# Retention's value projection: two 256-column units in one pass of 512-column products, with the weight loads and sums around it reordered

## What is computed

```python
c_act = jax.nn.silu(c)
for l in range(DEPTH):
    mod = c_act @ w_ada[l] + b_ada[l]          # adaLN: shift, scale, gate
    h = _modulate(_rmsnorm(x, norm_mix_g[l]), shift1, scale1)
    p = h @ w_in                               # rq, rk, rv, rg, ...
    ...
# per retention head: q, k are 256 wide, v and gate 512 wide
q, k = rotary(rq), rotary(rk)
scores = (q @ k.T) * decay                     # causal
o = scores @ v
o = (o - mean(o)) * rsqrt(var(o) + GN_EPS)
y_a = (silu(rg) * o) @ w_ret_out
```

## Time and profile before

| | before |
|---|---|
| median of 3 runs | 2310.23 us (2309.91 to 2310.75) |
| profiled execution, its own time | 2309.64 us |
| span from first to last instruction | 2307.9 us |
| PE busy | 2283.3 us, 99% |
| POOL busy | 1141.3 us, 49% |
| DVE busy | 1082.2 us, 47% |
| ACT busy | 906.9 us, 39% |
| DMA queue of SP, share of 16 engines | 33.4% |
| granted TensorE clock | 1.000 over the span |

### The profile page before, as it was taken

How to read it: one execution, slowest core, us unless ns; L and a number is a source line. 1 busy time by engine, 2 the same in 40 slices (tenths; PEclk the granted TensorE clock), 3 DMA queues, 4 the chain that set the end, 5 groups by cost and what they waited for, 6 DMA issues and landing times.

```text
span 2307.9 us, 30124 instructions
## 1 busy us (share of the span) xinstructions
PE 2283.3 (99%) x12146; PEld 1926.4 (83%) x12146; DVE 1082.2 (47%) x1497; ACT 906.9 (39%) x1093; POOL 1141.3 (49%) x1489
## 2 busy tenths in 40 slices
PE   7999999999999999999999999999999999999999
PEld 4888888888888888888898888888888788888887
DVE  5776657546653341121276766441666524221223
ACT  4332233256675242232343323232666834332332
POOL 3454544544454545555544455445444454545543
PEclk9999999999999999999999999999999999999999
DMA  9444534322222323323344544222222223233231
GB/s 301 133 154 144 182 118 146 128 74 74 74 92 73 98 95 95 106 92 92 110 134 134 162 133 146 85 84 92 74 74 74 73 91 92 93 100 100 92 95 70
DMA packets 244153, 252.48 MB, mean 109 GB/s; under 512 B 4016, under 2 KB 241728, under 8 KB 244032
## 3 DMA queue, kind: packets, MB, share of 16 engines
q1 hardware_dynamic: 242352, 247.00, 33.4%
q10 hardware_dynamic: 1680, 3.70, 0.5%
HBM read 248.59 MB, written 2.10 MB: 109 GB/s over the span
## 4 chain that ended last, share of the span: by engine, by line
PE 92%; DVE 4%; DMA 1%; SPq 1%; ACT 1%; issue 0%; DVEq 0%; ACTq 0%
PE proj L912 70%; PE proj L949 10%; PE att L1081 2%; PE proj L934 2%; PE att L1127 2%; PE att L1137 1%; PE att L1115 1%; DVE slab L1258 1%; PE proj L1010 1%; PE att L1061 1%; DVE att L1365 1%; SPq L316 1%; DVE h_lo L1372 1%; PE att L1090 1%; DMA slab<-in_w_ada 1%; DMA first_y<-in_w_ada 1%
## 5 line engine op out<-in xcount | busy, mean ns | idle before, releaser
L400 POOL TENSOR_TENSOR w_lo<-w_raw,w_hi 128x256 fp32r<-128x256 f32 x1472 | 1139.2, 806 | 1137.1 <-ACT w_hi L446 1136.5
L912 PE MATMUL proj<-h_hi,w_hi 128*128 128x512 f32 x1568 | 617.7, 394 | 0.3 <-DVE work L1453 0.2
L912 PE MATMUL proj<-h_hi,w_lo 128*128 128x512 f32 x1568 | 611.1, 390 | 0.0
L912 PE MATMUL proj<-h_lo,w_hi 128*128 128x512 f32 x1568 | 610.5, 389 | 0.0
L446 ACT ACTIVATE w_hi<-w_raw 128x1024 fp32r<-128x1024 f32 (+1 forms) x374 | 385.9, 1040 | 524.8 <-PE proj L912 438.6
L912 PEld LDWEIGHTS proj<-h_hi,w_lo 128*128 128x128 f32 x1568 | 294.4, 188 | 62.6
L912 PEld LDWEIGHTS proj<-h_hi,w_hi 128*128 128x128 f32 x1568 | 294.5, 188 | 62.2 <-issue 2.4
L912 PEld LDWEIGHTS proj<-h_lo,w_hi 128*128 128x128 f32 x1568 | 294.7, 188 | 58.6
L912 PE MATMUL proj<-y_hi,w_hi 128*128 128x512 f32 x800 | 311.3, 389 | 0.0
L912 PE MATMUL proj<-y_lo,w_hi 128*128 128x512 f32 x800 | 311.3, 389 | 0.0
L912 PE MATMUL proj<-y_hi,w_lo 128*128 128x512 f32 x800 | 311.2, 389 | 0.0
(11 more groups left out here) (231 smaller groups left out, 2456.7 us busy)
## 6 DMA issues: line engine op xcount, KB each, us to landing
w_raw<-in_w_in SPq DMA_DIRECT2D x88, 1024.0 KB, 5.1
slab<-in_w_ada SPq DMA_DIRECT2D x42, 1024.0 KB, 8.0
w_raw<-in_w_up SPq DMA_DIRECT2D x32, 1024.0 KB, 5.7
w_raw<-in_w_down SPq DMA_DIRECT2D x32, 1024.0 KB, 5.3
w_raw<-in_w_ret_out SPq DMA_DIRECT2D x16, 1024.0 KB, 5.5
w_raw<-in_w_sb_out SPq DMA_DIRECT2D x8, 1024.0 KB, 5.1
w_raw<-in_w_mix_out SPq DMA_DIRECT2D x8, 1024.0 KB, 5.2
first_y<-in_w_ada SPq DMA_DIRECT2D x4, 1024.0 KB, 12.6
```

The costliest lines, as they stand in the source:

```text
L400: ins = pool.tensor_tensor(w_lo[:, s, ks, :], w_raw[:, s // 2, ks, P * (s % 2):P * (s % 2 + 1)], w_hi[:, s, ks, :], ALU.subtract)
L912: last = pe.matmul(proj[:, j, :], w[:, slot, k, :], a[:, k, :], start=k == 0 and n == 0, stop=k == KT - 1 and n == 2)
```

## The change

1. **v in one pass** (`v_units`). The two v units are computed together: for each of the 8 row tiles and each of the 4 token blocks, three matmuls with all 512 weight columns of both units moving. There are 96 matmuls of 512 columns in place of 192 of 256. The four token blocks need a PSUM buffer each: blocks 0 and 1 go to `att[:, 4]` and `att[:, 5]`, blocks 2 and 3 to `proj[:, 0]` and `proj[:, 1]` (`v_of`).
2. **Weights in halves of rows.** The pass needs u+3 beside u+2, whose slot is k's (u+1) until then. So k is computed in two halves of the row tiles (`first_unit` with steps 4, 4), and after the first (`k_used`) ACT and POOL make the first half of u+3. The pass too tells when its first half of rows is done (`v_used`), and then the first half of u+4 is made. POOL's loop is written out, and its counts are in halves (`low_order`).
3. **v's split at the end.** ACT's four copies `v_hi` and DVE's four `low_v` stand behind the whole pass, in the order of blocks 2, 3, 0, 1. DVE's four slab sums stand in a row ahead of them. `add_ada` waits for the low parts of blocks 0 and 1 (`v_taken`).
4. **Loads.** Slabs 2 and 3 of a head are both asked for ahead of unit u+5. Before, u+5 stood between them.
5. **Rotation.** The second product has a buffer of its own (`rot_too`), so that it does not wait for the first sum.

The core of the diff:

```diff
-                            for k in ([], [], [], [0, 1], [2], [3])[n] if has_ada(layer, i, j) else []:
+                            for k in ([], [], [], [0, 1], [2, 3], [])[n] if has_ada(layer, i, j) else []:
...
+            def split_half(pair, unit, j, kh):
+
+                s = unit % 2
+                act.wait_ge(raw_in[s], 16 * (pair + unit // 2 + 1))
+                ks = K_HALVES[kh]
+                act.activation(w_hi[:, 2 * s + j, ks, :], w_raw[:, s, ks, P * j:P * (j + 1)],
+                               ACT.Copy).then_inc(hi_ready, 1)
...
+                        for kh in range(2):
+                            if kh == 0:
+                                act.wait_ge(k_used, head + 1)
+                            else:
+                                products(pair, u + 1, 1)
                             for half in range(2):
-                                products(pair, unit, half)
...
+                                split_half(pair, u + 3, half, kh)
...
+                        act.wait_ge(v_used, head + 1)
+                        for half in range(2):
+                            split_half(pair, u + 4, half, 0)
+                        products(pair, u + 3, 1)
+                        for half in range(2):
+                            split_half(pair, u + 4, half, 1)
+                        for t in (2, 3, 0, 1):
+                            act.activation(v_hi[:, t, :], v_of(t), ACT.Copy).then_inc(v_half, 1)
+                        for half in range(2):
+                            split_weights(pair, u + 5, half)
...
+            def v_units(pair, unit):
+
+                for kh in range(2):
+                    pe.wait_ge(lo_ready, 8 * pair + 4 * (unit + 1) + 2 * (kh + 1) + LO_CREDIT)
+                    for k in range(KH * kh, KH * (kh + 1)):
+                        for t in range(TB):
+                            if k == 0 and t in (0, 3):
+                                pe.wait_ge(bank_free[t // 2], 2 * pair + unit + 1)
+                            for n, (w, a) in enumerate(((w_hi, h_hi), (w_lo, h_hi), (w_hi, h_lo))):
+                                last = pe.matmul(v_of(t).rearrange("p (a n) -> p a n", a=4),
+                                                 a[:, k, t * P:(t + 1) * P], w[:, :, k, :],
+                                                 start=k == 0 and n == 0, stop=k == KT - 1 and n == 2)
+                            if k == KT - 1:
+                                last.then_inc(proj_done, 1)
+                    if kh == 0:
+                        last.then_inc(v_used, 1)
...
-                        whole_unit(pair, u + 1, h_hi, h_lo)
-                        token_unit(pair, u + 2)
-                        token_unit(pair, u + 3)
+                        first_unit(pair, u + 1, h_hi, h_lo, None, (KH, KH), k_used)
+                        v_units(pair, u + 2)
...
                         half_unit(pair, u + 4, 0, h_hi, h_lo)
+                        pe.wait_ge(v_taken, 2 * head + 2)
...
+                        def low_v(n, t):
                             dve.wait_ge(v_half, 4 * head + n + 1)
...
+                            dve.tensor_tensor(v_lo[:, t, :], v_of(t), v_hi[:, t, :], ALU.subtract
+                                              ).then_inc(*((v_taken, 1) if t < 2 else (bank_free[t - 2], 2)))
...
                         for q in range(4):
                             if has_ada(layer, i, h):
                                 sum_ada(layer, i, ADA_BATCH * h + q)
-                            low_v(q)
+                        for n, t in enumerate((2, 3, 0, 1)):
+                            low_v(n, t)
```

More of the change, by code:

```diff
@@ L76, with low_order @@
 BIG = 3.0e38
+RET_UNITS = 6
+KH = KT // 2
+WHOLE = slice(0, KT)
+K_HALVES = (slice(0, KH), slice(KH, KT))
+def low_order(layer):
+    order, pair = [], layer * LAYER_PAIRS
+    for unit in range(LAYER_UNITS):
+        head_unit = unit % (2 * RET_PAIRS) if unit < SB_FIRST else 2 * RET_UNITS
+        at = head_unit % RET_UNITS if head_unit < 2 * RET_UNITS else 0
+        order += [(unit, j, ks) for ks in (K_HALVES if at in (3, 4) else (WHOLE,)) for j in range(2)]
+    return order
 class Chain:
@@ L176, in hybrid_trunk @@
         rot = part(7680, SEQ)
+        rot_too = part(P_AT, SEQ)
         gated_t = rot
@@ L309, in load @@
                 s = unit % 2
-                sp.wait_ge(lo_ready, 4 * pair + 2 * unit - 2 + LO_CREDIT)
+                sp.wait_ge(lo_ready, 8 * pair + 4 * unit - 4 + LO_CREDIT)
                 sp.dma_start(w_raw[:, s:s + 1, :, :], src).then_inc(raw_in[s], 16)
@@ L903, in half_unit @@
                 slot = 2 * (unit % 2) + j
-                pe.wait_ge(lo_ready, 4 * pair + 2 * unit + j + 1 + LO_CREDIT)
+                behind = 1 if j == 0 and unit in (4, 4 + RET_UNITS) else 0
+                pe.wait_ge(lo_ready, 8 * pair + 4 * unit + 2 * (j + 1) + behind + LO_CREDIT)
                 pe.wait_ge(bank_free[j], 2 * pair + unit + 1)
@@ L918, in whole_unit, with first_unit @@
                     half_unit(pair, unit, j, hi, lo, tile_ready if j == 0 else None)
-            def first_unit(pair, unit, hi, lo, tile_ready, steps):
+            def first_unit(pair, unit, hi, lo, tile_ready, steps, used=None):
                 k0 = 0
@@ L937, in first_unit @@
                             last.then_inc(proj_done, 1)
+                        elif used is not None and j == 1:
+                            last.then_inc(used, 1)
                     k0 += step
+            def v_units(pair, unit):
[13 more added lines that the diff above has]
+                        last.then_inc(v_used, 1)
             def token_unit(pair, unit):
                 slot = 2 * (unit % 2)
-                pe.wait_ge(lo_ready, 4 * pair + 2 * unit + 2 + LO_CREDIT)
+                pe.wait_ge(lo_ready, 8 * pair + 4 * unit + 4 + LO_CREDIT)
                 for t in range(TB):
@@ L1454, in _ @@
                             products(pair, u + n, 1)
-                            own.link(dve.tensor_tensor(rot, proj[:, 1, :], rope_t[:, 1, :], ALU.mult))
+                            own.mark(dve.tensor_tensor(rot, proj[:, 1, :], rope_t[:, 1, :], ALU.mult))
+                            free(dve.tensor_tensor(rot_too, proj[:, 1, :], rope_t[:, 0, :], ALU.mult), 1)
+                            own.settle()
                             own.link(dve.tensor_tensor(a, a, rot, ALU.subtract))
-                            free(dve.tensor_tensor(rot, proj[:, 1, :], rope_t[:, 0, :], ALU.mult), 1)
-                            dve.wait_ge(bank_free[1], 2 * pair + u + n + 2)
-                            dve.tensor_tensor(b, b, rot, ALU.add).then_inc(qk_rotated, 1)
+                            taken(pair, u + n, 1)
+                            dve.tensor_tensor(b, b, rot_too, ALU.add).then_inc(qk_rotated, 1)
                             dve.wait_ge(qk_rotated, 2 * head + n + 1)
```

64 lines of the change are left out of this document (28 added, 36 removed).

## The result

The changed kernel takes 2324.42 us in the median of five runs (2319.49 to 2326.05), against 2309.91 (2309.16 to 2310.75) for the kernel before on the same chip. The ratio is 1.0058, with a 95% interval of 1.0046 to 1.0069. The prediction was 2314.2 with a range up to 2323: the direction held, the size did not. The profiled run took 2326.05 us, its span 2324.3, which is 16.4 us over the span of before.

What follows compares the result with a forecast made beforehand. PE bound the kernel, DVE level within about 0.3 us in heads with slab sums. Seven heads at +0.75 us (+5.3) and one at -1.3 gave +4.0 on the 2307.9 span; adding 1.7 and 0.6 gave 2314.2, range 2303 to 2323.

Steps and rivals of the forecast that it cites:

- The pass: v pass: 96 matmuls of 512 columns take 21.77 us against 23.07, saving 10.4 us over eight heads.
- rival D: v pass: four moving pieces still cost 23.07 us, nothing gained or lost, about 2310.5 us; chance 0.05.
- Weights in halves at no cost: u+3's first half is ready by about T-1.3 (T: start of the v pass); both halves cost nothing.
- Rival C: u+3's first half is late at the v pass's start; 1 us late in eight heads gives 2322; chance 0.05.
- The slab sums: DVE's sums take 3.90 us alone, 5.34 or 5.7 beside POOL; block 2's low part ends at T+27.65 (T: pass start).
- Slab 3: With u+5's load no longer ahead, it lands in 5.3 us instead of 6.8; DVE waits 1.4 us for it.
- DVE's own end: End of DVE's chain in a head, given as T+32.5 to T+33.5 (T: start of the v pass).
- The wait ahead of u+4: PE waits 2.1 us for proj[:, 0], until block 2's low part is done, in seven heads, not the last.
- The rest of u+4's half and the slab additions take 6.07 us: PE's work behind its new wait; scores by v then start at T+33.7, against T+32.92 (T: start of the v pass).
- Queued behind PE's new wait is all of the head's rest, which follows in step and pays no more: The rest of each head behind PE's new wait moves with it and adds no further cost.
- B: Slower, same buffer wait, dearer: slab 3 at 6.8 us gives 2332 at most, DVE 0.3 us late gives 2316; chance 0.35.
- A: PE waits nowhere, block 2's low part ending 2.1 us sooner; 2299.8 us; chance 0.13 together with a half-way case.

Runs made afterwards that it cites:

- fill_wait: The changed kernel with nine matmuls that nothing reads ahead of u+4's first half in the seven heads with slab sums; 2316.67 us, ratio 1.0028.
- covered_no_fill: The covered_credit kernel without its nine filling matmuls ahead of u+4's first half in the very first head; 2303.81 us, ratio 0.9974.
- short_sum: The changed kernel with the fourth slab sum of each head cut to its first instruction; 2300.27 us, ratio 0.9955.
- early_sum: The changed kernel with each head's first slab sum moved ahead of k's rotation, except in the very first head; 2310.12 us, ratio 1.000.
- early_sum_loads: The early_sum kernel with slabs 0 and 1 also asked for ahead of u+3's weights, except in the very first head; 2308.74 us, ratio 0.9993.
- old_loads: The changed kernel with u+5's weights asked for between slabs 2 and 3 again; 2337.87 us, ratio 1.0116.
- fill_part: The fill_wait kernel with four filling matmuls in place of nine; 2317.10 us, ratio 1.0032.
- covered_credit: The covered kernel with DVE giving layer 1's slab-load credit after layer 0's second norm, not on entering layer 1; 2302.05 us, ratio 0.9967.
- covered: The early_sum_loads kernel with layer 1's first slabs asked for sooner, a later buffer wait, and nine filling matmuls in the very first head; 2316.29 us, ratio 1.0029.

## Why the prediction was right in its mechanism and wrong in its size

- **The pass.** Taken at 21.77 us on the floor of 228 ns; measured 21.75, and 9.4 to 10.4 us in all. Four moving pieces cost nothing (rival D falls).
- **Weights in halves at no cost.** u+3's first half was ready at T-1.9 (266.46 + 2.83) against T-1.3 predicted, and no pass of the changed kernel waits on POOL. Rival C falls.
- **The slab sums.** First 3.90 against 3.90; the second 5.36 (281.51 to 286.87) against 5.34; POOL's starts at T+11.6 and T+22.5 as worked out. The fourth took 5.35 in this head and 5.86 in the first, against 5.7, so block 2 was done at T+27.0 here, against T+27.65, and u+4's half could start at T+27.8 in five heads (88.42 less 60.65).
- **Slab 3.** 5.1 us to landing against 5.3, and DVE waited 1.28 us for it against 1.4. In the seventh head it took 6.0 us, and DVE waited 2.17: hence PE's 3.2 us there.
- **A sum that was added up wrongly.** DVE's own end was given as T+32.5 to T+33.5. The terms beside it, from block 2's low part at T+27.65, give T+33.2 to T+34.1. DVE ended at T+33.1 in the third head (301.48 + 2.83) and T+33.2 in the first, and PE waited for it in no head, so nothing came of the slip.
- **The wait ahead of u+4.** Predicted 2.1 us in seven heads and none in the last; measured 2.26 in five heads, 1.65 in the third, 3.2 in the seventh: 16.2 in place of 14.7. The place, the releaser and the count are right; this term was 1.5 us short.
- **The step that failed** is "The rest of u+4's half and the slab additions take 6.07 us", together with "Queued behind PE's new wait is all of the head's rest, which follows in step and pays no more". The 6.07 us was read where PE had not stopped, and was carried to a place where it had. It takes 7.8 to 7.9 us there in five of seven heads, because for part of that time the clock is at its lower level; the prediction puts a cost of the clock at nothing without naming it. Scores by v start at T+35.7 in the first head (96.35 less 60.65), not at T+33.7. That is 9.4 us in the profiled run, the slowest of the five, and most of the 10.2 by which the median was missed; fill_wait and covered_no_fill show it apart.
- **The rivals.** B had the right sign and a range that takes in the result, but its causes are not what happened: slab 3 did not take 6.8 us in any head, and block 2's low part was at most 0.1 us later than forecast in six of the seven. A number that is met by another cause is no confirmation. A needed block 2's low part 2.1 us sooner; short_sum shows that this would indeed have given 2300.

One thing stays open: what decides whether the clock falls. Of the waits ahead of u+4's first half in the profiled runs, it fell behind six of eight of 2.3 us (four of five in the changed kernel, none in early_sum, one each in early_sum_loads and covered_no_fill), behind seven of eight of 3.1 us and more (the seventh head, and six of seven in old_loads), and behind none of eight of 0.7 to 1.65 us (the third head, and seven in fill_part). So a longer wait makes it likelier, and the runs don't show what else has a part in it. Nor does it fall at a fixed moment: in the changed kernel's first head some 1.5 us after PE resumed, in old_loads' third head already at the first matmul, which takes 0.76 us instead of 0.47.

This also fits the spread of the changed kernel, whose five runs differ by 6.6 us, where covered_credit's six differ by 2.0. The mean granted clock of each run is known: it was 0.998 in the fastest, 0.995 in the slowest, and fell in between as the time rose. A drop of 0.003 over 2320 us means an estimated 14 us more at the lower level, which costs half of that, 7 us.

## What to carry to other kernels

Price a new wait on the engine that bounds the kernel twice: its idle time, and the clock of what runs behind it. A duration read where the engine was busy holds only as long as the engine stays busy. When a saving makes the bound engine reach a shared buffer sooner, list all that the other engine does ahead of freeing it, and shorten that queue in the same change; here the pass alone lost 14.5 us, the earlier sum and loads alone gained nothing, and together, with the credit given sooner and one wait filled, they gained 7.9 us. Where the wait can't be removed, a few matmuls that compute nothing, put into it, cost next to nothing and held the clock here.

## What the runs showed of the hardware

- Idle stretches of PE of 2.3 us lowered the granted clock to 0.5 in four heads of the changed kernel and in the first heads of covered_no_fill and early_sum_loads, one of 3.2 us in the seventh head. The 24 matmuls behind took 1.7 to 1.9 us longer than 5.50. Two stretches of 2.3 us (the fifth head, and early_sum's first) and one of 3.12 us (old_loads) did not lower it, nor did those of 1.65 us (third head) and of at most 1.3 us (fill_part). Where the clock fell behind the waits of old_loads, of 3.1 to 5.6 us, the cost was 1.8 to 3.1 us each.
- Behind a wait with the clock at 1.00 throughout, the same 24 matmuls took 5.69 to 5.73 us.
- A matmul whose 512 moving columns come in four pieces of 128 runs at the speed of one piece: six in 1.36 us, 227 ns each. Two of 256 columns cost 240 ns (twelve in 1.44 us).
- A load of 1 MB took 5.1 us to land with nothing ahead of it (6.0 in the seventh head), and 9.8 and 11.3 us at the start of layer 1 (early_sum's slab, covered's weights), where other loads were under way.
